# Cached values multiplied four pages at a visit in the four column quarters, the second recurrence begun three ticks later, and two steps of VectorE reordered

## The chip, the core and the metric
The kernel runs on one core of a Trainium2 chip. TensorE (matrix products), VectorE, ScalarE and GpSimd compute, SyncE issues the DMAs, and all five run their own instruction streams and wait for each other by semaphores. The metric is the time of the whole launch on the device in microseconds (us), the median of several runs.

## What is computed
One step of a hybrid decoder layer, for a prompt of 1024 tokens and for 8 running sequences (samples) with one new token each. Both go through a combined input projection, a gated linear recurrence (4 heads, in blocks), a differential attention (4 heads, two query and key pairs each), an output projection and a feed-forward with squared relu. The change concerns the samples' attention over their cached values:

```python
def diff_attn_sample(q, k_new, v_new, k_past, v_past, lam):
    # q, k_new (Bd,1,H,2,DH); v_new (Bd,1,H,DV); k_past (Bd,P,H,2,DH); v_past (Bd,P,H,DV)
    s_past = einsum('bqhcd,bkhcd->bhcqk', q, k_past) * scale
    s_new = einsum('bqhcd,bkhcd->bhcqk', q, k_new) * scale
    p = softmax(concatenate([s_past, s_new], -1))
    a = p[:, :, 0] - lam * p[:, :, 1]
    return (einsum('bhqk,bkhv->bqhv', a[..., :P], v_past)
            + einsum('bhqk,bkhv->bqhv', a[..., P:], v_new))

k_past = cache_k[l, page_table].reshape(Bd, past, H_DIFF, 2, DH_DIFF)
v_past = cache_v[l, page_table].reshape(Bd, past, H_DIFF, DV_DIFF)
```

There are 8 sequences of 16 pages, a page is 128 positions of 512 numbers (256 KB), so 128 pages of values are fetched through the page table and multiplied by the softmax's coefficients.

## The kernel before
**Main line.** Everything is float32; dense products are split into high and low parts and done as three products each (`split_matmuls`, L85 to L87). The `front` computes the input projection in groups (kinds dq, low, gk, gq, gv, dk, dv, gg; nine groups for a kind of 512 columns: eight token tiles and the samples). Then `feed_forward` runs for the first half of the tokens (part A: output projection, then eight groups of four up tiles and eight down outputs), then for the second half (part B). For part A TensorE has two PSUM banks for its dense results, so it can't begin an output before VectorE has taken the one two places earlier (for down outputs that is the residual addition, L2195).

**Ticks.** Main work is cut into ticks. In the front a token tile is two ticks, a sample tile one. In feed-forward A an output tile and an up tile are two ticks and each of the eight down outputs is one; up tile x of group g holds the ticks 16 + 16g + 2x and the next, and the down outputs start at tick 24 + 16g. Every engine walks the same ticks in order, and at each calls `beside(tick)`, which runs one step of each side job that the table in `program` (L2801 to L2835) has put there, in the order of the `put` lines. So an engine's instruction order is fixed by hand, and an engine that waits inside a side step holds up its main work behind it. In a down product TensorE does its first two outputs and then both first ticks' side work together (L1976 to L1983), while VectorE does each tick's side work ahead of the addition of that output (L2189 to L2195).

**Side jobs that matter here.** `recurrence` (parts A and B, 4 chunks of 9 phases each, one phase a tick): VectorE subtracts decays in phases 0 and 1, multiplies in phases 3 to 5 (`multiply(c, 0..2)`, L1165), and copies masked scores out of PSUM in phases 5 to 7 (`pick(c, 0..2)`, L1183); TensorE does the score levels in phases 5, 6 and 7 (L1284), of which phase 6 waits for pick 0 and the second multiply and phase 7 for pick 1 and the third multiply, and sums outputs in phase 8, after pick 2. `cached_keys` (`keysA`, `keysB`): SyncE fetches key pages, GpSimd multiplies them with the queries (L2338), VectorE sums (L2327). `sample_recurrence`, then `sample_softmax` (L2344), then `cached_values` (L2456), which starts as the softmax ends. In the front, `sample_normed("dk")` (L794) norms the samples' keys on VectorE after GpSimd has taken the roots; SyncE stores them to `k_sample` (L331) and waits for that norm, two groups behind.

**Cached values.** A unit is two pages. SyncE fetches one unit a step into a ring of three slots (L2207). TensorE visits it two steps later: two products of 128 x 32 coefficients (`a_pad`, four heads padded to 32 columns) with 512 columns of values, in quarters g and g + 1 of the array's columns (L2550 to L2552), so the quarters' sums stand in the partitions 32g to 32g + 31 of one bank. Eight units are one sequence. After them VectorE masks the bank (L2530, `vm`), TensorE adds it over the partitions by a product with ones (`total`, L2538), and VectorE adds the row to `acc_s` (L2515).

## Time and profile before
| | |
|---|---|
| three runs | 1525.34 us median (1522.49 to 1526.05) |
| profiled execution, whole | 1533.14 us |
| its span, first to last instruction | 1531.2 us |
| mean granted TensorE clock | 0.971 of full |
| busy: TensorE products, VectorE, ScalarE, GpSimd | 94%, 56%, 35%, 21% |
| cached-value products, L2551 | 256 records, 769.8 to 1055.5 us |
| DMA | 212 MB, 138 GB/s over the span |

Times inside an execution are microseconds from its first instruction. PE is TensorE, PEld its weight loads, DVE VectorE, ACT ScalarE, POOL GpSimd, SPq the DMA issues of SyncE. A float32 product of two unsplit operands leaves two records. Products are pipelined and their ends are modelled, so records overlap and starts tell more than durations. The profiled execution is one of the kernel, and its time is compared with itself.

### The profile page before, as it was taken

How to read it: one execution, taken by the hardware profiler on the slowest of the kernel's cores; microseconds unless marked ns; L12 is line 12 of the kernel's file. 1: busy time of each engine (PE TensorE's matmuls, PEld its weight loads, DVE VectorE, ACT ScalarE, POOL GpSimd, SP SyncE). 2: the span in 40 equal slices, each digit the busy share in tenths (PEclk: the TensorE clock that was granted, in tenths of full speed). 3: DMA queues.
4: the chain of work that ended last, by engine and by line, in shares of the span. 5: the costliest groups of instructions: out<-in, count | busy, mean ns of one | idle time of the engine just before them, and what ended most of it. 6: DMA issues, size and time to landing. Idle time of an engine off the chain costs nothing.

```text
span 1531.2 us, 23353 instructions
## 1 busy us (share of the span) xinstructions
PE 1438.9 (94%) x8649; PEld 1165.9 (76%) x8649; DVE 857.8 (56%) x1438; ACT 533.5 (35%) x980; POOL 324.6 (21%) x366
## 2 busy tenths in 40 slices
PE   6998899889999989999899999999899999999997
PEld 5767677667776767876666665556899999999997
DVE  4467667744647776786746472425255544455542
ACT  5462232314545564520413140303244322233321
POOL 2456624523412523464000000000030000000000
PEclk9999999989999999999899999999999999999999
DMA  7547644434244532463437464844153312233211
GB/s 240 152 145 210 209 140 151 131 115 119 71 144 134 162 130 90 161 220 116 156 112 246 140 227 133 296 138 152 49 177 120 106 63 81 83 110 111 102 38 57
DMA packets 115635, 211.99 MB, mean 138 GB/s; under 512 B 12665, under 2 KB 45722, under 8 KB 115522
## 3 DMA queue, kind: packets, MB, share of 16 engines
q1 hardware_dynamic: 115522, 210.50, 42.4%
q8 instruction: 69, 1.13, 0.3%
q14 instruction: 44, 0.36, 0.1%
HBM read 184.00 MB, written 26.46 MB: 137 GB/s over the span
## 4 chain that ended last, share of the span: by engine, by line
PE 66%; DVE 5%; ACT 2%; issue 2%; DMA 1%; SPq 0%; ACTq 0%; DVEq 0%
PE ps L85 18%; PE ps L87 17%; PE ps L86 17%; PE ps L2551 4%; PE ps L1465 2%; PE ps L1502 2%; PE ps L1284 1%; DVE uw_l L2038 1%; PE ps L1486 1%; DMA out_y_prompt<-y 1%; ACT uw_h L2034 1%; DVE dl L2126 0%; PE ps L2612 0%; PE ps L2538 0%; PE ps L1692 0%
## 5 line engine op out<-in xcount | busy, mean ns | idle before, releaser
L85 PE MATMUL ps<-uh,dh 128*128 128x512 f32 (+2 forms) x768 | 253.8, 330 | 18.1 <-DVE dl L2126 10.6
L87 PE MATMUL ps<-uh,dl 128*128 128x512 f32 (+2 forms) x768 | 248.5, 324 | 0.0
L86 PE MATMUL ps<-ul,dh 128*128 128x512 f32 (+2 forms) x768 | 247.9, 323 | 0.0
L2338 POOL TENSOR_TENSOR kr<-kr,qb 128x512 f32<-128x512 f32 x128 | 174.3, 1378 | 123.7 <-DMA kr<-in_cache_k 119.7
L2195 DVE TENSOR_TENSOR xt<-xt,ps 128x256 f32<-128x256 f32 (+2 forms) x192 | 97.2, 511 | 167.0 <-PE ps L87 166.2
L85 PEld LDWEIGHTS ps<-uh,dh 128*128 128x128 f32 x768 | 146.2, 190 | 46.9 <-DVE xt L2195 22.3
L2049 ACT ACTIVATE dh<-raw_dn 128x1024 fp32r<-128x1024 f32 x64 | 67.1, 1049 | 266.2 <-PE ps L87 263.3
L87 PEld LDWEIGHTS ps<-uh,dl 128*128 128x128 f32 x768 | 146.2, 190 | 12.1
L86 PEld LDWEIGHTS ps<-ul,dh 128*128 128x128 f32 x768 | 146.6, 191 | 10.0
L85 PE MATMUL ps<-x2hB,uw_h 128*128 128x264 f32 (+1 forms) x512 | 145.9, 285 | 3.2 <-DVE uw_l L2038 2.6
L2034 ACT ACTIVATE uw_h<-raw_up 128x1024 fp32r<-128x1024 f32 x80 | 84.4, 1055 | 182.8 <-PE ps L87 182.7
L86 PE MATMUL ps<-x2lB,uw_h 128*128 128x264 f32 (+1 forms) x512 | 145.2, 284 | 0.0
L87 PE MATMUL ps<-x2hB,uw_l 128*128 128x264 f32 (+1 forms) x512 | 145.0, 283 | 0.0
L2038 DVE TENSOR_TENSOR uw_l<-raw_up,uw_h 128x1024 fp32r<-128x1024 f32 x80 | 101.6, 1270 | 43.1 <-ACT uw_h L2034 43.1
L85 PE MATMUL ps<-x2hA,uw_h 128*128 128x512 f32 x256 | 106.9, 418 | 0.0
L87 PE MATMUL ps<-x2hA,uw_l 128*128 128x512 f32 x256 | 101.3, 396 | 0.0
L86 PE MATMUL ps<-x2lA,uw_h 128*128 128x512 f32 x256 | 100.9, 394 | 0.0
L85 PEld LDWEIGHTS ps<-x2hB,uw_h 128*128 128x128 f32 x512 | 97.2, 190 | 3.7 <-DVE uw_l L2038 2.8
L2327 DVE TENSOR_REDUCE sd<-kr 128x8 f32<-128x512 f32 x128 | 84.7, 675 | 25.3 <-POOL kr L2338 25.2
L86 PEld LDWEIGHTS ps<-x2lB,uw_h 128*128 128x128 f32 x512 | 97.1, 190 | 0.0
L87 PEld LDWEIGHTS ps<-x2hB,uw_l 128*128 128x128 f32 x512 | 96.9, 189 | 0.0
L2126 DVE TENSOR_TENSOR dl<-raw_dn,dh 128x1024 fp32r<-128x1024 f32 x64 | 80.3, 1254 | 27.3 <-ACT dh L2049 27.2
(327 smaller groups left out, 2888.0 us busy)
## 6 DMA issues: line engine op xcount, KB each, us to landing
kr<-in_cache_k SPq DMA_DIRECT2D x128, 256.0 KB, 3.2
raw_up<-in_w_up_units SPq DMA_DIRECT2D x64, 512.0 KB, 3.7
raw_dn<-in_w_down SPq DMA_DIRECT2D x64, 512.0 KB, 4.6
vr<-in_cache_v SPq DMA_DIRECT2D x128, 256.0 KB, 3.1
raw<-in_w_in_units SPq DMA_DIRECT2D x24, 512.0 KB, 5.1
raw_up<-in_w_out_units SPq DMA_DIRECT2D x16, 512.0 KB, 3.6
xin<-in_x_prompt SPq DMA_DIRECT2D x8, 512.0 KB, 5.5
xt_scratch<-xts SPq DMA_DIRECT2D x8, 512.0 KB, 5.8
```

Of the source, the lines that this page charges most:

```text
L85: pe.matmul(out, lh, rh, start=first and n == 0, stop=False)
L86: pe.matmul(out, lh, rl, start=False, stop=False)
L87: ins = pe.matmul(out, ll, rh, start=False, stop=last and n == len(ks) - 1)
L1465: pe.matmul(ps[:, score_bank(n, c) + j // 512, 0:x], qt[r, b, i * P:(i + 1) * P], kt[r, b, j:j + x], start=True, stop=j + x < w)
L2034: act.activation(uw_h[:, t % 2, :, :], raw_up[:, t % 2, :].rearrange("p (k c) -> p k c", c=P), ACT.Copy).then_inc(up_high, 1)
L2038: dve.tensor_tensor(uw_l[:, t % 2, :, :], raw_up[:, t % 2, :].rearrange("p (k c) -> p k c", c=P), uw_h[:, t % 2, :, :].bitcast(FP32), ALU. ...
L2049: act.activation(dh[:, x, :], raw_dn[:, x % 2, :], ACT.Copy).then_inc(dn_high, 1)
L2126: dve.tensor_tensor(dl[:, x, :], raw_dn[:, x % 2, :], dh[:, x, :].bitcast(FP32), ALU.subtract).then_inc(dn_low, 1)
L2195: dve.tensor_tensor(xt[:, o, c], xt[:, o, c], ps[:, bank("down", g, o, p), 0:spans[p][1]], ALU.add).then_inc(added, 1)
L2327: dve.tensor_reduce(m["sd"][:, b, g, :], place(v)[:, :].rearrange("p (h d) -> p h d", d=DH), X, ALU.add).then_inc(k_used, 1)
L2338: pool.tensor_tensor(k[:, :], k[:, :], qb[v // PAGES][:, :], ALU.mult).then_inc(k_multiplied, 1)
L2551: ins = pe.matmul(ps[32 * g:32 * g + 32, 2 + b % 2, :], a_pad[:, b % 2, 2 * l + j, :], vring[v % VRING][:, j, :], start=l < 2, stop=l >= 6 ...
```

## The change
`cached_values` fetches and visits four pages at a time. A unit is now four pages, 32 units in all, in a ring of eight single-page places. SyncE fetches two pages of a unit at an even step and two at the following odd step; TensorE visits a unit at step 2u + 3 with four products, one in each quarter; masking, total and addition stand at steps 10, 11 and 12 + 8b instead of 9, 10 and 10 + 8b. The places of the ring reach over memory that other jobs used, so SyncE waits for three more things before it starts and, before page 7, for the softmax's last step. The job has 69 steps instead of 68.

In `recurrence`, both parts, the third multiply moves behind the first pick of the same phase. In the front, the norm of the samples' keys moves from the first to the second group of dv. In the table the tail of `keysB` is spread over 16 ticks instead of 15, the softmax and values start one tick later, and `recurB` starts 13 ticks after the softmax's start instead of 10, with its first load 10 instead of 7 after; counted from the feed-forward's start recurB begins at tick 72 instead of 68. Two places in memory move by 64 bytes. The diff, with the moved memory places left out:

```diff
--- before.py
+++ after.py
@@ -889,7 +889,7 @@
                     gkq_sample(g)
             if g in (START["gg"] + 3, START["gg"] + 4):
                 m["late"]["vector"](dve, g - START["gg"] - 3)
-            if x == 0 and kind in ("low", "dv"):
+            if kind == "low" and x == 0 or kind == "dv" and x == 1:
                 sample_normed("dq" if kind == "low" else "dk")
             if ticks_of(g) == 2:
                 beside(TICK[g] + 1)
@@ -1219,10 +1219,12 @@
             if ph == 2 and c > first:
                 finish(c - 1)
             if here:
-                if 3 <= ph < 6:
+                if 3 <= ph < 5:
                     multiply(c, ph - 3)
                 if 5 <= ph < 8:
                     pick(c, ph - 5)
+                if ph == 5:
+                    multiply(c, 2)
             yield
 
     def scalar(act):
@@ -2200,15 +2202,9 @@
 
-VALUE_UNITS = NS * PAGES // 2
+VALUE_UNITS = NS * PAGES // 4
 KEY_PAGES = NS * PAGES // 2
-VRING = 3
-
-
-def load_unit(sp, cache, m, slot, arrived, first):
-    for j in range(2):
-        page = sp.value_load(m["pages"][0:1, first + j:first + j + 1], min_val=0, max_val=NPOOL - 1)
-        sp.dma_start(slot[:, j, :], cache[bass.ds(page, 1), :, :].rearrange("a p n -> p (a n)")).then_inc(arrived, 16)
+VRING = 2
 
@@ -2455,7 +2451,9 @@
 
 def cached_values(nc, a, m, ps, sem, at):
 
-    vring = [at(f"vr{i}", 166.625 + 4 * i, [P, 2, W]) for i in range(VRING)]
+
+    places = [164.6875 + 2 * i for i in range(7)] + [202.625]
+    vring = [at(f"vr{i}", x, [P, W]) for i, x in enumerate(places)]
     a_pad = at("a_pad", 9.75, [P, 2, PAGES, 32])
     hmask = at("hmask", 1.5, [P, W])
     vm = at("vm", 162.6875, [P, W])
@@ -2466,17 +2464,26 @@
     keys_in = [16 * len([v for v in range(2 * KEY_PAGES) if key_sem(v) == i]) for i in range(VRING)]
     v_used, v_masked, v_totalled, v_added, padded = (sem(x) for x in ("v_used", "v_masked", "v_totalled", "v_added", "padded"))
     sums = m["head_sums"][:, 0:H]
-    STEPS = VALUE_UNITS + 4
+    STEPS = 2 * VALUE_UNITS + 5
 
     def sync(sp):
         sp.wait_ge(sem("scored"), 4 * UNITS)
         sp.wait_ge(sem("product_made"), 2 * UNITS)
         sp.wait_ge(sem("k_used"), 2 * KEY_PAGES)
+        for i in range(3):
+            sp.wait_ge(sem(f"od_out{i}"), (96, 80, 80)[i])
+        sp.wait_ge(sem("st_updated"), 1)
         for s in range(STEPS):
-            if s < VALUE_UNITS:
-                if s >= VRING:
-                    sp.wait_ge(v_used, s - VRING + 1)
-                load_unit(sp, a["cache_v"], m, vring[s % VRING], v_in[s % VRING], 2 * s)
+            u, j = divmod(s, 2)
+            if u < VALUE_UNITS:
+                if j == 0 and u >= VRING:
+                    sp.wait_ge(v_used, u - VRING + 1)
+                for v in (4 * u + 2 * j, 4 * u + 2 * j + 1):
+                    if v == 7:
+                        sp.wait_ge(v_added, 1)
+                    page = sp.value_load(m["pages"][0:1, v:v + 1], min_val=0, max_val=NPOOL - 1)
+                    sp.dma_start(vring[v % 8][:, :], a["cache_v"][bass.ds(page, 1), :, :].rearrange("a p n -> p (a n)"))\
+                        .then_inc(v_in[u % VRING], 16)
             yield
 
     def gpsimd(pool):
@@ -2503,12 +2510,12 @@
                     dve.wait_ge(sem("coef_made"), 1)
                     dve.wait_ge(sem("fill_steps"), 6)
                 if b >= 2:
-                    dve.wait_ge(v_used, 8 * (b - 1))
+                    dve.wait_ge(v_used, 4 * (b - 1))
                 dve.tensor_copy(a_pad[:, b % 2, :, 0:H], coef[:, b, :, :]).then_inc(padded, 1)
-            b, j = divmod(s - 9, 8)
+            b, j = divmod(s - 10, 8)
             if j == 0 and 0 <= b < NS:
                 v_masked_now(dve, b)
-            b, j = divmod(s - 10, 8)
+            b, j = divmod(s - 12, 8)
             if j == 0 and 0 <= b < NS:
                 dve.wait_ge(v_totalled, b + 1)
                 dve.wait_ge(v_added, b + 1)
@@ -2524,7 +2531,7 @@
                           sums.unsqueeze(2).to_broadcast([NS, H, DV]), ALU.mult).then_inc(sem("ods_done"), 1)
 
     def v_masked_now(dve, b):
-        dve.wait_ge(v_used, 8 * (b + 1))
+        dve.wait_ge(v_used, 4 * (b + 1))
         if b:
             dve.wait_ge(v_totalled, b)
         dve.tensor_tensor(vm[:, :], ps[:, 2 + b % 2, :], hmask[:, :], ALU.mult).then_inc(v_masked, 1)
@@ -2538,20 +2545,19 @@
             pe.matmul(ps[0:NS, 2 + b % 2, :], m["ones"][:, 0:NS], vm[:, :], start=True, stop=True).then_inc(v_totalled, 1)
 
         for s in range(STEPS):
-            v = s - 2
-            if 0 <= v < VALUE_UNITS:
-                b, l = divmod(v, 8)
-                pe.wait_ge(v_in[v % VRING], keys_in[v % VRING] + 32 * (v // VRING + 1))
+            u, j = divmod(s - 3, 2)
+            if j == 0 and 0 <= u < VALUE_UNITS:
+                b, l = divmod(u, 4)
+                pe.wait_ge(v_in[u % VRING], keys_in[u % VRING] + 64 * (u // VRING + 1))
                 if l == 0:
                     pe.wait_ge(padded, b + 1)
                     if b >= 2:
                         pe.wait_ge(v_added, b)
-                for j in range(2):
-                    g = (2 * l + j) % 4
-                    ins = pe.matmul(ps[32 * g:32 * g + 32, 2 + b % 2, :], a_pad[:, b % 2, 2 * l + j, :],
-                                    vring[v % VRING][:, j, :], start=l < 2, stop=l >= 6, tile_position=(0, 32 * g))
+                for g in range(4):
+                    ins = pe.matmul(ps[32 * g:32 * g + 32, 2 + b % 2, :], a_pad[:, b % 2, 4 * l + g, :],
+                                    vring[(4 * u + g) % 8][:, :], start=l == 0, stop=l == 3, tile_position=(0, 32 * g))
                 ins.then_inc(v_used, 1)
-            b, j = divmod(s - 10, 8)
+            b, j = divmod(s - 11, 8)
             if j == 0 and 0 <= b < NS:
                 total(b)
             yield
@@ -2824,13 +2830,13 @@
         put("attnB", [t0 + i for i in range(ATTEND_STEPS + 1) if i != norm])
         late = t0 + ATTEND_STEPS + 1
         put("keysB", [t0 + 2 + 41 * i // 25 for i in range(25)])
-        put("keysB", [late + 15 * i // (side["keysB"]["steps"] - 25) for i in range(side["keysB"]["steps"] - 25)])
-        t1 = late + 15
-        put("loadRB", [t1 + 7])
+        put("keysB", [late + 16 * i // (side["keysB"]["steps"] - 25) for i in range(side["keysB"]["steps"] - 25)])
+        t1 = late + 16
+        put("loadRB", [t1 + 10])
         put("sgla", [late + 1 + i * 3 // 2 for i in range(side["sgla"]["steps"])])
         put("soft", range(t1, t1 + side["soft"]["steps"]))
         put("values", range(t1 + 12, t0 + FEED_TICKS))
-        put("recurB", range(t1 + 10, t1 + 10 + side["recurB"]["steps"]))
+        put("recurB", range(t1 + 13, t1 + 13 + side["recurB"]["steps"]))
         put("mixload", [t1 + 54])
         put("mixB", [t0 + 137 + i // 2 for i in range(9)])
 
```

## Rows read from the trace of the kernel before
**Rows 1.** The page: the chain that ended last, by line.
```profile
PE ps L85 18%; PE ps L87 17%; PE ps L86 17%; PE ps L2551 4%; PE ps L1465 2%; PE ps L1502 2%; PE ps L1284 1%; DVE uw_l L2038 1%; PE ps L1486 1%; DMA out_y_prompt<-y 1%; ACT uw_h L2034 1%; DVE dl L2126 0%; PE ps L2612 0%; PE ps L2538 0%; PE ps L1692 0%
```

**Rows 2.** TensorE's waits over the span: us in total, times, longest us.
```profile
PE ps L1284 <- DVE at_sb L1193: 13.1, 2, 8.6
PE ps L85 <- DVE dl L2126: 10.6, 2, 6.8
PE ps L85 <- DVE xt L2195: 7.9, 5, 2.9
```

**Rows 3.** The chain in order of time, feed-forward A: start us, us, what.
```profile
769.91 0.99 PE ps L2551 x8
1018.65 0.98 PE ps L2551 x4
1022.61 0.98 PE ps L2551 x4
```

**Rows 4.** Timeline of TensorE at a down product's first ticks, 844 to 852 us.
```profile
844.90 0.40 PE L85 MATMUL ps<-uh,dh 128*128 128x512 f32 x1
...
845.61 0.39 PE L85 MATMUL ps<-uh,dh 128*128 128x512 f32 x1
...
846.39 1.07 PE L2551 MATMUL ps<-vr,a_pad 128*32 128x512 f32 x8
847.27 1.02 PE L2538 MATMUL ps<-vm,ones 128*8 128x512 f32 x2
851.18 0.51 PE L85 MATMUL ps<-uh,dh 128*128 128x512 f32 x1 [2.88 <-DVE xt L2195]
```

**Rows 5.** Windows: busy by engine, then PEclk, DMA share, GB/s.
```profile
186.00:197.00 11.00, 8.19 (x43) 7.13 (x44) 5.10 (x10) 0.00 (x0) 0.60 (x1) 0.53 0.47 135
...
306.30:319.80 13.50, 9.07 (x46) 7.36 (x46) 7.24 (x14) 0.00 (x0) 1.29 (x1) 0.50 0.35 100
...
757.00:767.00 10.00, 5.43 (x13) 4.28 (x14) 7.08 (x19) 5.43 (x6) 0.95 (x1) 0.50 0.71 229
...
852.40:855.70 3.30, 3.30 (x10) 2.05 (x11) 2.15 (x9) 0.00 (x0) 0.00 (x0) 0.50 0.71 234
...
964.00:996.00 32.00, 32.00 (x132) 19.70 (x131) 15.55 (x18) 11.70 (x15) 0.00 (x0) 1.00 0.84 296
```

**Rows 6.** Timeline of VectorE before the down product at 761 us.
```profile
754.94 1.76 DVE L1151 TENSOR_TENSOR e<-g_in 128x256 f32<-128x256 f32 x5
...
760.28 1.23 DVE L2126 TENSOR_TENSOR dl<-raw_dn,dh 128x1024 fp32r<-128x1024 f32 x1 [1.46 <-ACT dh L2049]
```

**Rows 7.** Timeline of VectorE in the front, recurrence chunks 0 and 3.
```profile
184.44 2.31 DVE L1177 TENSOR_TENSOR e<-e,g_in 128x128 f32<-128x128 f32 x2
...
302.29 4.18 DVE L798 TENSOR_TENSOR zs<-zs,zsum 8x512 f32<-8x512 f32 x1 [1.55 <-POOL zsum L683]
306.51 1.63 DVE L800 TENSOR_TENSOR zs<-zs,gains 8x512 f32<-8x512 f32 x1
```

**Rows 8.** Timeline of GpSimd, 302 to 308 us.
```profile
302.23 5.36 POOL L2338 TENSOR_TENSOR kr<-kr,qb 128x512 f32<-128x512 f32 x4
```

**Rows 9.** Timeline of VectorE in chunk 2 of the front's recurrence.
```profile
260.38 0.49 DVE L1177 TENSOR_TENSOR e<-e,g_in 128x128 f32<-128x128 f32 x2
...
261.12 0.73 DVE L1191 COPY_PREDICATED at_sb<-lmask,ps 128x512 f32<-128x512 int32 x1
261.89 0.94 DVE L1193 COPY_PREDICATED at_sb<-lmask,ps 128x256 f32<-128x256 int32 x2
```

**Rows 10.** Timeline of GpSimd at the same time.
```profile
261.09 2.53 POOL L2338 TENSOR_TENSOR kr<-kr,qb 128x512 f32<-128x512 f32 x2
```

**Rows 11.** Value page fetches (L2211), 770 to 1056 us: who waited; landing.
```profile
  PEld ps L2551: 0.4, 1
...
DMA to landing us min/median/max: 2.5/3.1/5.6
```

**Rows 12.** Timeline of ScalarE, fifth group of dv.
```profile
340.93 0.69 ACT L561 ACTIVATE st<-ps,r 128x512 f32<-128x512 f32 x1 [10.58 <-DMA out_v_prompt<-st]
```

More of the change, by code:

```diff
@@ L1032, in recurrence @@
     first, last = CHUNKS * part, CHUNKS * (part + 1)
-    base = (166.625, 178.625)[part]
+    base = (166.625, 178.6875)[part]
     g_in = at(f"g_in{part}", base, [P, 3, 2, P])
@@ L1633, in mixing @@
         tiles = [(t, half) for t in range(4) for half in range(2)] + [(4, 0), (4, 1)]
-        rowsB = at("rowsB", 178.625, [P, MIX_RING, W])
+        rowsB = at("rowsB", 178.6875, [P, MIX_RING, W])
     else:
```

## The prediction
> **What bounds the kernel now.** I read the page first. The chain that ended last is mostly TensorE's: its split products at L85 to L87 and then, at 4% of the span, the cached-value products at L2551 [rows 1]. So a microsecond of TensorE's own work is worth a microsecond, if nothing else is late. Next I read TensorE's waits, to see where it stands still [rows 2]. Three kinds touch the change: two waits of the recurrence's score products on the predicated copies of VectorE (13.1 us, the longest 8.6), two waits on the split of the down weights (10.6 us, the longest 6.8), and waits on VectorE's residual additions (7.9 us). The windows then show what each wait costs beyond itself: behind the long ones the granted clock is 0.50, the lower of its two levels (1.2 of 2.4 GHz), while TensorE works [rows 5].
>
> **Four pages at a visit.** Before, 64 units of two pages are visited. In four places, at the first two ticks of a down product, two units are visited back to back, so there are 60 stretches. Two neighbouring single visits start 3.96 us apart [rows 3] with twelve dense products between. Three dense products take 0.71 us, from 844.90 to 845.61 [rows 4], and twelve 2.81, so a visit takes 1.15 us: 0.98 on the chain [rows 3], and 0.17 for entering and leaving it. After the change there are 32 visits of four. Their price stands in the trace: a back-to-back pair of units touches all four quarters (l even: quarters 0 and 1, then 2 and 3), and its eight records run from 846.39 to 847.27, 0.88 us until the next product starts [rows 4]. Another such place, 769.91, had 0.99 on the chain [rows 3]. I take 1.00. The work itself falls from 60 x 0.98 = 58.8 to 32.0 us. Entering and leaving is paid once per tick that has side work. Before, each of the 60 is such a tick. After, I count 32 visits, 8 ticks with a recurrence step alone and one total alone: 41. That saves 19 x 0.17 = 3.2 us. Term one: -30.0 (bounds -27 and -31).
> The Trainium skill speaks against the full price: TensorE: Matmul & The Clock Gate, section Measured speedup vs the span model, lists 3.07x for four row tiles and 2.38x for three column tiles of 512 columns, and says that the two tilings agree closely. By that, four together would take 1.30 times one product alone; with this case's single product (0.85 us) a visit would cost 1.11, and the change would save 3.5 us less. The rows above are of this kernel, and the sum goes by them.
>
> **The totals move off the boundary.** A tick is half an up tile or one of the eight outputs of a down product, 12 dense products each. Values started at tick 70 of the feed-forward and start at 71; VectorE adds batch b's total at step 12 + 8b instead of 10 + 8b. A down product's first tick is 72 + 16k. Before, odd b lands there exactly: VectorE sits in the wait for TensorE's total before it does the first residual addition, and TensorE, with two banks, can't go on: 2.88 us at 851.18 [rows 4], two more of 2.7 and 1.4 in the sum of rows 2, with 0.4 at the end. After the first the clock is at half for 3.3 us [rows 5], after the second as long: 1.7 lost each time. After the change steps 20, 36 and 52 are ticks 91, 107 and 123, inside the down product, and only the masking (step 18, 34, 50) falls on its second tick, with a whole product of cover. Gain 7.4 + 3.4 = 10.8.
> But TensorE does both first ticks of a down product together, and the moved recurrence (first step at tick 72, before 68) now has steps 32 and 33 there (phases 5 and 6 of its last chunk): phase 6 waits for the first pick, three predicated copies of 0.73 and 0.94 us together [rows 9], with nothing between: 1.8. Steps 16 and 17 (phases 7 and 8) wait for one short copy: 0.4. The total of even b comes one tick after a masking that stands behind VectorE's work on an up tile: 0.1 to 0.3 each. Term two: -10.8 + 2.8 = -8.0 (-5 to -9).
>
> **Recurrence away from the softmax.** Before tick 72 VectorE has the last softmax steps, the recurrence's first two (five of their subtractions alone take 1.76 us), and ScalarE has the exponentials of those, in front of the last down split, which ends at 761.5 [rows 6]; TensorE waits 6.8 us and then runs 5.4 us at half clock, 2.7 lost [rows 2, 5]. After, softmax ends at tick 71 and the recurrence starts at 72, so some 5 us of VectorE's work and two exponentials leave the way to the split. Rebuilt with the same durations the split ends within 0.3 us of TensorE's need. What is late next: the last softmax step, a weight split and the recurrence's first step stand before the first residual addition. With that tile's own steps they are about 8 us (2.2 + 2.2 + 1.2 + 1.7 + 0.7), and TensorE has two outputs of 2.8 us of products to cover them: a new stall of 2.6, perhaps with some half clock. Term three: -9.5 + 2.6 + 0.9 = -6.0 (-3 to -9). SyncE's new waits cost nothing: the stored rows and the state update ended long before, and the wait at page 7 for the softmax's last sum comes two ticks after it with no weight load behind it for six ticks.
> **Keys over 16 ticks instead of 15.** By tick 54 VectorE has made two reductions fewer (0.68 us each) before the other split on which TensorE waits, for 3.8 us (10.6 less 6.8 [rows 2]); the half clock that follows may shorten. Term four: -2.0 (0 to -4).
>
> **The last multiply behind the first pick.** In phase 5 of both recurrences TensorE's phase 6 needs the pick, and the last multiply only phase 7. In chunk 0 the multiply stands first and takes 2.31 us for two instructions [rows 7] that take 0.49 elsewhere [rows 9]; with its last part (0.4 us) that is 2.6 ahead of the pick, which could start at 184.44. A pick isn't slowed by GpSimd's products: at 261.12 it takes its 0.73 beside them [rows 9, 10]. TensorE's wait of 4.5 (13.1 less 8.6) falls to 2.0. Behind it 8.19 us of work ran at 0.53 [rows 5], 4.1 lost; a wait of 2.0 may or may not lower the clock, I take half. Term five: -2.6 - 2.4 = -5.0 (-2.6 to -6.7).
> **The samples' key norm one group later.** It stood in front of the pick of chunk 3. Its two instructions took 4.18 and 1.63 us [rows 7], beside GpSimd's four key products, 5.36 us [rows 8]. TensorE waited 8.6, and ran 9.07 us at 0.50, 4.5 lost [rows 2, 5]: 13.1. After: the pick ends near 302.4 (wait 0.3). The multiply now meets GpSimd's products and, priced by 4.18 for one such instruction at worst, ends by 306.3 to 308.3; a reduction and the second pick (2.17) follow, and phase 7 waits 2 to 4 us. With 3.0 for that and 1.7 for some half clock, 5.0 is lost instead of 13.1. Term six: -8.0 (-4 to -11). SyncE now waits for this norm with the store of the samples' keys, until about 311 to 312 instead of 308; it is priced as a rival.
>
> **Sum.** 30 + 8 + 6 + 2 + 5 + 8 = 59. The profiled execution took 1533.1 us (span 1531.2), so 1474 for one like it; the three runs have a median of 1525.3, 7.8 below, and the same difference gives 1466.
>
> **The rivals.**
> (a) Four streams don't run together when they start at once, and a visit of four costs two products. For: each quarter needs its own stream of 512 columns. Against: rows 4. Price 32 x 0.9 = 29: 1495.
> (b) The front doesn't keep its 13 us. SyncE stays in the norm's wait; behind it stand a key store, a page load and the value store whose landing ScalarE already waited for once, 10.6 us until 340.93, which cost TensorE 1.9 [rows 12]. For: TensorE arrives 8 us earlier, SyncE 3 later. Against: that later wait hangs on the recurrence's end, which moves along. 1479.
> (c) The softmax stall comes back in full, at the first residual addition: 1466 + 8 = 1474.
> (d) Slower: the visit waits for its second pair of pages. SyncE issues it a tick later than the first, behind its waits for the weight splits, and the visit comes two ticks after. Landing takes 3.1 us, at most 5.6 [rows 11]; the up stages already use 0.84 of the DMA engines at 296 GB/s [rows 5], and shorter ticks want about a sixth more. I count about 5 us of slack. The gain is gone once every one of 32 visits waits 59 / 32 = 1.85 us, so from a lateness of about 7 us on; with 2.2 us each it is 1466 + 70 = 1536. Against: before, with the same two pages a tick, the visits waited 0.4 us in all for pages [rows 11].
>
> **How the numbers follow.** Forecast 1466, chance 0.63, with 1454 to 1478 as its own range from the terms' bounds; (c) 0.12; (b) 0.13; (a) 0.06; (d) 0.03; the rest, smaller give-backs up to no change, 0.03. The range to 1486 takes in (c) and (b) and leaves out (a), (d) and the rest. A measurement can tell about 0.3% (4.6 us) from no change. Faster 0.96, same 0.01, slower 0.03.
>
> **What would show it.** L2551 in 32 places with eight records each, the next product 0.9 to 1.0 us after the first; no wait of L85 on the residual addition near the middle of the feed-forward but one of under 2 us where the recurrence's phases 5 and 6 meet; the wait on the down split after the softmax gone, a shorter one on the addition behind it; the waits on the predicated copies at 2 and at under 4 us; fewer windows at 0.50. Visits near 1.9 us would prove (a); waits of L2551 on the pages (d); a longer wait of ScalarE's L561 on the value store (b).

## The result and the profile after

| | kernel before | changed kernel |
|---|---|---|
| median | 1525.69 us (1522.49 to 1530.10, 4 runs) | 1490.01 us (1484.83 to 1492.57, 4 runs) |
| ratio | | 0.976, 95% interval 0.972 to 0.980 |
| profiled execution, whole | 1533.14 us | 1487.50 us |
| its span | 1531.2 us | 1485.6 us |

The change is faster by 36 us. The forecast was 1466 with a range to 1486, so the sign is right and the time lies outside the range. Between the two profiled executions 45.6 us went, where the sum had 59. The medians differ by less, 36 us, because the profiled execution of the kernel before was 7.8 us above its median and that of the changed kernel 2.5 below. So the miss is 13 us in the traces and 23 us in the medians; both are taken apart below.

The new kernel's lines stand a few places off: L2557 is the cached-value product (L2551 before), L2197 the residual addition, L2128 the split of the down weights, L1286 the recurrence's score product, L2485 the page fetch.

First the visits. TensorE's timeline around one of them (start us, us, what), which answers to [rows 3, 4]:

```profile
930.12 0.40 PE L87 MATMUL ps<-x2hA,uw_l 128*128 128x512 f32 x1
930.45 1.06 PE L2557 MATMUL ps<-vr,a_pad 128*32 128x512 f32 x8
931.45 0.50 PE L85 MATMUL ps<-x2hA,uw_h 128*128 128x512 f32 x1
```

Four pages hold the stream for 1.00 us, as priced. TensorE's waits over the span (us in total, times, longest us) answer to [rows 2]:

```profile
PE ps L1286 <- DVE at_sb L1193: 7.2, 4, 3.1
...
PE ps L2557 <- DMA vr<-in_cache_v: 6.0, 3, 4.1
...
PE ps L85 <- DVE dl L2128: 4.1, 2, 2.8
PE ps L85 <- DVE xt L2197: 4.1, 3, 2.9
```

The waits on the predicated copies fell from 13.1 to 7.2, those on the down split from 10.6 to 4.1, those on the residual addition from 7.9 to 4.1. The line of L2557 is new: 6.0 us of waiting for value pages, where there were 0.4 [rows 11]. What the waits drag behind them is in the windows (from:to, us, busy by engine with counts, then PEclk, DMA share, GB/s), which answer to [rows 5]:

```profile
181.00:190.00 9.00, 7.00 (x48) 5.43 (x46) 5.91 (x13) 0.69 (x1) 2.48 (x2) 0.81 0.51 135
301.00:309.50 8.50, 5.44 (x25) 4.03 (x24) 7.25 (x13) 1.63 (x2) 0.21 (x1) 0.69 0.19 41
...
805.80:816.00 10.20, 7.84 (x40) 5.25 (x41) 3.57 (x13) 1.33 (x2) 0.00 (x0) 0.51 0.95 356
898.00:904.80 6.80, 6.30 (x38) 5.67 (x39) 4.75 (x11) 0.00 (x0) 0.00 (x0) 0.51 0.46 147
964.00:996.00 32.00, 32.00 (x152) 20.54 (x150) 10.96 (x16) 4.22 (x5) 0.00 (x0) 1.00 0.58 171
```

Two new stretches at the lower clock level (0.51) stand in the feed-forward, at 806 and at 898 us. To find where the 45.6 us came from, I cut both traces at the same pieces of work, the starts of named additions on VectorE. Worked out from the records: length of the stage, and in brackets how long TensorE had nothing running, then half of what it ran at half clock (what the half clock cost).

```
                      start to      part A, g0 o4   g2 o4 to       g3 o4 to        to the end of
                      g0 o4         to g2 o4        g3 o4          end of part A   TensorE's work
before                593.5 (75.9)  129.3 ( 7.9)    64.0 (6.8,2.7) 297.6 ( 7.4,3.4) 439.4
changed               581.4 (62.7)  126.9 ( 5.3)    54.0 (4.6,1.7) 280.2 (10.1,7.2) 437.8
changed, once more    581.3 (62.5)  127.1 ( 5.5)    56.6 (4.6,4.6) 280.7 ( 9.7,8.2) 438.0
```

(The first two columns have both losses in one number; "g3 o4" is the fifth down output of the fourth group. Some of the recurrence's own work moved from the third column to the fourth with its start.) In the feed-forward's part A, TensorE's work without the losses went from 462.7 to 432.2, by 30.5 us: that is the visits. Its losses went from 28.2 to 28.9, where the prediction took 16 off. That is where the traces' 13 us are missing: 16.7 here, of which 3.3 came back elsewhere.

Not all of the 45.6 us belong to the change. Two runs below have one half of the kernel before each. The four pages alone have the old front, and their trace reaches g0 o4 after 588.8 us with 70.8 lost, against 593.5 with 75.9; their waits on the predicated copies there were 3.2 and 7.0 us, where the trace that the prediction read had 4.5 and 8.6. The norm alone has the old code behind the front, and takes 443.4 us from the end of part A to the end of the span, where the kernel before takes 446.7 and the changed one 443.1. So about 8 us of what the profiled execution of the kernel before lost, it lost in stretches where the same code lost less in another execution.

### The profile page after: what moved, and what is told of

The parts are those of the page before. It is cut to its first block, busy times and chain, and to the rows that moved or that the text cites. A ratio compares the mean times of both kernels' runs of the same rounds, so it can differ in the third digit from the quotient of the medians.

```text
span 1485.6 us, 23355 instructions
## 1 busy us (share of the span) xinstructions
PE 1406.0 (95%) x8649; PEld 1161.6 (78%) x8649; DVE 857.0 (58%) x1438; ACT 533.8 (36%) x980; POOL 324.3 (22%) x366
## 4 chain that ended last, share of the span: by engine, by line
PE 63%; DVE 6%; ACT 3%; issue 2%; DMA 1%; SPq 1%; POOL 0%; ACTq 0%; DVEq 0%; POOLq 0%
PE ps L85 18%; PE ps L87 17%; PE ps L86 17%; PE ps L1467 2%; PE ps L2557 2%; PE ps L1504 2%; PE ps L1286 1%; DVE uw_l L2040 1%; PE ps L1488 1%; DMA vr<-in_cache_v 1%; ACT uw_h L2036 1%; DMA out_y_prompt<-y 1%; DVE dl L2128 1%; PE ps L2618 0%; PE ps L2010 0%
## 5 line engine op out<-in xcount | busy, mean ns | idle before, releaser
L2197 DVE TENSOR_TENSOR xt<-xt,ps 128x256 f32<-128x256 f32 (+2 forms) x192 | 97.4, 511 | 157.9 <-PE ps L87 157.3
L2036 ACT ACTIVATE uw_h<-raw_up 128x1024 fp32r<-128x1024 f32 x80 | 84.5, 1056 | 172.8 <-PE ps L87 172.7
L2128 DVE TENSOR_TENSOR dl<-raw_dn,dh 128x1024 fp32r<-128x1024 f32 x64 | 81.6, 1275 | 27.9 <-ACT dh L2051 27.7
L2179 DVE SCALAR_TENSOR_TENSOR xr<-ps,rb 128x256 f32<-128x256 f32 (+1 forms) x96 | 49.0, 514 | 83.1 <-PE ps L87 82.8
```

What stands on the lines that cost most here:

```text
L2036: act.activation(uw_h[:, t % 2, :, :], raw_up[:, t % 2, :].rearrange("p (k c) -> p k c", c=P), ACT.Copy).then_inc(up_high, 1)
L2128: dve.tensor_tensor(dl[:, x, :], raw_dn[:, x % 2, :], dh[:, x, :].bitcast(FP32), ALU.subtract).then_inc(dn_low, 1)
L2179: dve.scalar_tensor_tensor(vt[:, i % 2, 0:spans[p][1]], ps[:, bank("up", g, x, p), 0:spans[p][1]], 0.0, rb2[:, tokens(p)], ALU.max, ALU.mu ...
L2197: dve.tensor_tensor(xt[:, o, c], xt[:, o, c], ps[:, bank("down", g, o, p), 0:spans[p][1]], ALU.add).then_inc(added, 1)
```

## The long wait near 808 us

SyncE's issues in the changed kernel (start us, us, what):

```profile
792.92 1.77 SPq L2485 DMA_DIRECT2D vr<-in_cache_v  x2
800.37 0.33 SPq L1117 DMA_DIRECT2D kept_og<-go  x1
800.75 0.43 SPq L1831 DMA_DIRECT2D raw_up<-in_w_up_units  x1
801.22 0.45 SPq L1843 DMA_DIRECT2D raw_dn<-in_w_down  x1
802.42 1.45 SPq L2485 DMA_DIRECT2D vr<-in_cache_v  x2
```

VectorE and TensorE at the same place:

```profile
799.59 0.75 DVE L1207 SCALAR_TENSOR_TENSOR go<-gate,hr,go 128x512 f32<-128x512 f32 x1
...
808.16 1.94 PE L2557 MATMUL ps<-vr,a_pad 128*32 128x512 f32 x8 [4.14 <-DMA vr<-in_cache_v]
```

A unit's first two pages are issued at 792.9, its other two at 802.4. Between them SyncE stands in the wait of the recurrence's store (L1117, phase 2) for the gated rows `go`, which VectorE ends at 800.34; SyncE goes on at 800.37. The waits of SyncE from 790 to 806 us name it (us, times, longest):

```profile
SPq L1117 <- DVE go L1207: 5.7, 1, 5.7
```

TensorE was ready at 804.0. Before the change this store fell on tick 79; the recurrence's start, four ticks later, puts it on tick 83, between the two halves of a unit. This is theory S. The store's wait itself is not new. The trace of the kernel before, from 770 to 1060 us, has it at three of the four stores, up to 7.7 us long, and it did no harm there, since both pages of a unit were issued in one step:

```profile
SPq L1117 <- DVE go L1207: 18.1, 3, 7.7
```
 The rival, D, is that the DMA engines are simply full there (0.95 of them busy, 356 GB/s), and pages would be late whatever SyncE did.

## Experiments

The kernel before ran on the same chip beside them: its medians were 1527.3 us for the first four kernels, 1528.0 for the next four (two quarters, the parts alone) and 1527.9 for the last four. Times of one kernel scatter by up to 7 us about the median, so differences of medians under about 3 us tell nothing, and there the traces are compared.

### The changed kernel once more, and the store moved

> The changed kernel once more, as the level for the three runs beside it: 1490, ratio to before 0.976. In its trace the pages of one visit are waited for 4.1 us near 808 us, behind SyncE's wait of 5.7 us for the gated rows of the recurrence (L1117), and 8.5 us are lost to half clock and 9.9 to standing still between 762 and 1042 us.

Measured: 1491.73 us, ratio 0.9753 (0.9731 to 0.9774). Its trace has the same pages missing (6.0 us in 3 waits, the longest 3.4), 9.7 us idle and 8.2 us of half clock in the table's stage from g3 o4 to the end of part A.

```diff
-            if part and ph == 3 and here:
+            if part and ph == 5 and here:
                 ... (waits, then the gate's load)
-            if part and ph == 2 and c > first:
+            if part and c > first and (ph == 5 and here or ph == 2 and not here):
                 sp.wait_ge(og_gated, c)
                 sp.dma_start(a["og"][(c - 1) * P:c * P, :], go[:, :]).then_inc(go_out, 16)
```

> The changed kernel, with SyncE's store of the recurrence's gated rows and the load of the next gate (phases 2 and 3) moved to phase 5. Theory S: the second pair of pages came late at 808 us because SyncE stood 5.7 us in the wait of that store, which the later start of the recurrence moved to tick 83, between the two pairs of a unit. Then the wait of 4.1 us and the half clock behind it (5.1 us) go: 9 us less than after_again, 1481. Rival D: the pages are late because the DMA engines are full there (360 GB/s, share 0.99); then the wait stays at 3 to 4 us and the time is the same, 1489 to 1491.

Measured: 1482.15 us, ratio 0.9697 (0.9679 to 0.9714), 9.6 less than the changed kernel beside it. The window over that place, and the visit in it:

```profile
801.00:811.00 10.00, 9.99 (x65) 7.24 (x64) 9.57 (x26) 5.40 (x7) 0.00 (x0) 1.00 0.90 325
```
```profile
805.85 1.07 PE L2557 MATMUL ps<-vr,a_pad 128*32 128x512 f32 x8
```

No wait, full clock, and the DMA engines nearly as busy as in the changed kernel (0.90, 325 GB/s). The stage from up tile x2 of group 4 to the third down output behind it took 22.3 us instead of 30.1. Rival D falls as the cause of the long wait. But there was nothing to spare either: the last page of that unit was issued at 801.82, landed at 805.80, and the visit began at 805.85. The landings of this pair took 4.0 and 4.4 us, those of the changed kernel 4.6 and 4.7, against a median of 3.1 before the change [rows 11]. The prediction had counted some 5 us of slack at each visit.

### All four pages at the even step

```diff
-                for v in (4 * u + 2 * j, 4 * u + 2 * j + 1):
+                for v in range(4 * u, 4 * u + 4) if j == 0 else ():
```

> The changed kernel, with all four pages of a unit issued at the even step instead of two and two, so that they stand ahead of the store's wait in SyncE's order and ahead of the next weight loads. Theory S: the wait at 808 us goes, and the small ones of 0.7 and 1.2 us at 883 and 946 too, each with its half clock where it has some: 9 to 11 us less than after_again, 1480. Rival D: four pages in one burst fill the DMA engines as much, and delay weights: no gain, 1489 to 1492, perhaps with new waits for raw_up or raw_dn.

Measured: 1479.06 us, ratio 0.9672 (0.9651 to 0.9694), 12.7 less. The store's wait is still there (5.1 us near 800 us), but the pages stand ahead of it. TensorE's waits from 760 to 1050 us:

```profile
PE ps L85 <- DVE dl L2128: 2.0, 1, 2.0
PE ps L1286 <- DVE at_sb L1193: 1.9, 1, 1.9
PE ps L85 <- DVE xt L2197: 1.2, 2, 0.7
```

Not one wait for a page is left. So two different edits, one that moves the wait and one that moves the pages, both take the long wait away, and the second takes the two smaller page waits (0.7 to 1.5 us near 885 and 948) as well. No store stands between the halves of those two units, and the run with the moved store kept both waits (0.6 and 2.1 us); what made their pages late is not shown beyond this, that an earlier issue removes it.

### The recurrence back at tick 68

```diff
-        put("loadRB", [t1 + 10])
+        put("loadRB", [t1 + 6])
-        put("recurB", range(t1 + 13, t1 + 13 + side["recurB"]["steps"]))
+        put("recurB", range(t1 + 9, t1 + 9 + side["recurB"]["steps"]))
```

> The changed kernel, with the second recurrence (and its first load) begun at tick 68 of the feed-forward as in the kernel before, instead of 72; all else stays. Theory S: the softmax's stall comes back (6.8 us and half clock, 7 to 8 us net of the residual wait of 2.9 that goes), but the store's wait falls on tick 79 again, so the pages at 808 us are on time (9 us less), and phases 5 and 6 no longer share a down product's first ticks (1.9 us and 3.4 us of half clock less): in sum 6 us less, 1484. As the prediction had it (shift worth 6, its price 2.8): 3 us more, 1493.

Measured: 1483.55 us, ratio 0.9701 (0.968 to 0.9721), 8.2 less than the changed kernel. Its waits from 735 to 1050 us:

```profile
PE ps L85 <- DVE dl L2128: 6.2, 1, 6.2
PE ps L2557 <- DMA vr<-in_cache_v: 3.2, 2, 1.8
PE ps L85 <- DVE xt L2197: 2.8, 3, 1.5
PE ps L2368 <- DVE small L2409: 1.8, 1, 1.8
```

The softmax's stall is back (6.2 us at 753.76), and the stage with it takes 62.6 us instead of 56.6; but the stages behind it take 265.4 instead of 280.7. The store falls on tick 79 again. That is between the two halves of a unit too, but SyncE found its rows ready there. The third store, at tick 97, is between halves and did wait, 5.9 us, and the visit of that unit waited for its pages:

```profile
872.22 0.33 SPq L1117 DMA_DIRECT2D kept_og<-go  x1
874.27 1.44 SPq L2485 DMA_DIRECT2D vr<-in_cache_v  x2
879.00 1.07 PE L2557 MATMUL ps<-vr,a_pad 128*32 128x512 f32 x8 [1.39 <-DMA vr<-in_cache_v]
```

So the harm needs both, a place between the halves and a result that is late; and it still depends on TensorE: the changed kernel's third store waited 5.4 us between the halves at 885 us, and the visit, at 893.7, found its pages there.

The two places where the shift loses can be told apart in their stages: 7.8 us near 808, by the run with the moved store, and near 900 (from the third up tile to the fifth down output of group 5) losses of 7.2 us where there are none with the recurrence at 68. There the recurrence's phases 5 and 6 share the down product's first two ticks. So the part of the change that the prediction valued at 6 us of gain, 3.2 after the 2.8 that it charged in its totals' term, cost 8.

### Two quarters instead of four

```diff
+                    q = g if l == 0 else g % 2
-                    ins = pe.matmul(ps[32 * g:32 * g + 32, ...], ..., start=l == 0, stop=l == 3, tile_position=(0, 32 * g))
+                    ins = pe.matmul(ps[32 * q:32 * q + 32, ...], ..., start=l == 0, stop=(l == 3 and g > 1) or (l == 0 and g > 1),
+                                    tile_position=(0, 32 * q))
```

> The changed kernel, with the last three visits of every four putting their four pages in two quarters (0, 1, 0, 1) instead of four; the sums over the partitions come out the same. If the price of a visit is set by the columns each quarter has to take, 24 visits cost about 1.85 us instead of 0.995: 20 us more than the changed kernel, 1512. If it is set by the issue of eight records or by entering and leaving the tick, nothing changes: 1491.

Measured: 1501.87 us, ratio 0.9827 (0.9805 to 0.9849), 10 more than the changed kernel. A visit of this kernel in two quarters, with the product behind it:

```profile
937.21 1.91 PE L2558 MATMUL ps<-vr,a_pad 128*32 128x512 f32 x8
939.05 0.50 PE L85 MATMUL ps<-x2hA,uw_h 128*128 128x512 f32 x1
```

1.84 us instead of 1.00, in 24 places: 20.2 us of work, so rival (a) of the prediction is refuted by what its world looks like. The time rose by half of that only. The losses behind the fifth down output of group 3 fell from 17.9 to 10.3 us: slower visits leave SyncE and the pages more time, and the long wait near 810 was 2.3 instead of 3.4 us with a shorter half clock. That reading is not tested by itself; it would be the effect that took gain from the change, seen from its other side.

### The parts alone

```diff
-            if x == 0 and kind in ("low", "dv"):
+            if kind == "low" and x == 0 or kind == "dv" and x == 1:
```

> The kernel before with one edit: the norm of the samples' keys one group of dv later. The prediction priced it at 8.0 us, between 4 and 11; by the trace of the changed kernel (waits of 8.6 and the half clock behind them against 0.3 and 3.1) it is worth 6.3: 1521 against 1527. Rival (b) of the prediction: SyncE and the store of the prompt's values give it back, the wait of ScalarE at 340 us grows by as much: 1527, no change.

Measured: 1517.64 us, ratio 0.9922 (0.9898 to 0.9945), 10.4 less than before: more than the trace of the changed kernel had. At the place of the 8.6 us a wait of 1.03 is left, with no half clock behind it:

```profile
301.43 1.78 PE L1284 MATMUL ps<-e 64*128 64x64 f32 x28 [1.03 <-DVE at_sb L1193]
301.00:311.00 10.00, 9.57 (x78) 7.97 (x79) 7.01 (x12) 1.63 (x2) 5.18 (x5) 1.00 0.40 137
```

The wait of ScalarE for the value store is 10.60 us as before [rows 12], so rival (b) is refuted.

> The kernel before with one edit: the third multiply behind the first pick, in both recurrences. The prediction priced it at 5.0 us, between 2.6 and 6.7; by the trace of the changed kernel 4.8: 1522.5 against 1527. Rival: it is given back at the next wait that has another cause (the front's norm, 8.6 us at 302 us, grows): 1527.

(The diff is the part of the change in `recurrence`.) Measured: 1521.64 us, ratio 0.995 (0.9933 to 0.9968), 6.4 less than before. The wait of chunk 3, 8.57 us before, is 7.83 here, not longer (in the trace of the next run, whose front is that of the kernel before, it is 7.03), so the rival finds no support.

> The changed kernel without the two reordered steps of VectorE and with the second recurrence begun at tick 68: only four pages at a visit, the ring, the totals' steps and the table's one tick. By the prediction's terms one, two (without its new stall of 2.8) and four: 30 + 10.8 + 2 = 43 us less than before, 1484. By the run with the recurrence at 68, whose stages give 33 us from the middle of the feed-forward on: 33 to 36 us less, 1492 to 1494; the waits for pages (3.2 us) and for a residual addition (1.5) then stand where the totals' waits stood.

(The changed kernel with `sample_normed`, `multiply` and the start of recurB as before.) Measured: 1492.38 us, ratio 0.977 (0.9748 to 0.9792), 35.6 less than before. The sum of the terms, 43, lies outside the interval (32 to 38 us). Its trace has waits that had no place in that sum: for pages 1.5 and 1.3 us, for a residual addition 1.5, in the softmax 1.8, 6.1 us in all.

Alone, the three give 10.4 + 6.4 + 35.6 = 52.4; together, with the recurrence at tick 68, 43.8. The norm and the multiply, worth 16.8 alone, add 8.2 to the four pages (10.5 by the ratios, each uncertain by 4 to 5). Two of the parts hinder each other, and VectorE's timelines show where. Chunk 3 of the front's recurrence in the changed kernel, with GpSimd beside it:

```profile
295.37 0.92 DVE L1193 COPY_PREDICATED at_sb<-lmask,ps 128x256 f32<-128x256 int32 x2
296.19 5.18 DVE L1177 TENSOR_TENSOR e<-e,g_in 128x128 f32<-128x128 f32 x2
```
```profile
296.18 5.03 POOL L2334 TENSOR_TENSOR kr<-kr,qb 128x512 f32<-128x512 f32 x4
```

The same with the norm's edit alone, where the multiply stands ahead of the pick:

```profile
298.87 0.48 DVE L1177 TENSOR_TENSOR e<-e,g_in 128x128 f32<-128x128 f32 x2
299.28 0.41 DVE L1180 TENSOR_TENSOR e<-e,g_in 128x256 f32<-128x256 f32 x1
299.61 0.72 DVE L1191 COPY_PREDICATED at_sb<-lmask,ps 128x512 f32<-128x512 int32 x1
```

Behind the pick, the two instructions start together with GpSimd's key products and take as long as these, 5.18 us instead of 0.48; TensorE waits 3.1 us for the pick that follows, where 1.03 are left with the norm's edit alone. Ahead of it they are done before GpSimd begins. With the half clock behind the 3.1 (1.7 to 3.4 us) that makes 4 to 5 us of what the two lose in company; the rest is within the uncertainty. The Trainium skill has the rule in SBUF — State Buffer, section SBUF: two separate sides: a VectorE instruction with both inputs in SBUF and a GpSimd instruction that reads SBUF shut each other out for a whole instruction. These rows agree in that VectorE was shut out and the copies from PSUM were not. But it was for more than one instruction: by the single records VectorE's first took 3.88 us, over three of GpSimd's, its second 1.38, and GpSimd's own took 1.26 to 1.33 throughout.

### Putting the pieces together

Four kernels, each the changed kernel with more of the edits. First the recurrence three ticks later still, at 75:

```diff
-        put("loadRB", [t1 + 10])
+        put("loadRB", [t1 + 13])
-        put("recurB", range(t1 + 13, t1 + 13 + side["recurB"]["steps"]))
+        put("recurB", range(t1 + 16, t1 + 16 + side["recurB"]["steps"]))
-        put("mixload", [t1 + 54])
+        put("mixload", [t1 + 57])
```

> The changed kernel, with the second recurrence (and its first load) three ticks later again, at tick 75, and the load behind it three ticks later. Theory S: the store's wait falls on tick 86 behind both pairs of a unit, so the pages at 808 us are on time (8 us less); no chunk has phases 5 and 6, or 6 and 7, in a down product's first two ticks, so the wait of 1.9 us at 900 us goes with its half clock and the small wait before it (7.5 us less, as in the run at tick 68); and the residual wait of 2.3 to 2.9 us behind the softmax loses the recurrence's first steps (1 to 2 us less): 1474 to 1476. Rival: what matters is only that the recurrence overlaps the values' pages, wherever it stands; then one of the waits stays in another place and the time is 1482 to 1486.

Measured: 1480.96 us, ratio 0.97 (0.9676 to 0.9724), 5 above what was expected. The stage of the softmax behaved (52.2 us, 4.6 lost), the wait of 1.9 us near 900 is gone; but a wait of 2.8 us for a down split stands at 807 us, one of 1.5 for a residual addition at 887, and pages are waited for 3.3 us. The rival was half right: the recurrence's steps meet something wherever they stand. (Its profiled execution, 1476.25 us, was 4.7 below the median, so the trace shows less than was lost.)

> recur_at_75 with all four pages of a unit issued at the even step. Theory S: what page waits are left in recur_at_75 (2 to 3 us, as in the run at 68 and in the one with the later store) go: 2 to 3 us less than recur_at_75, 1472. Rival D: nothing, as a burst of four lands as late.

Measured: 1477.0 us, ratio 0.9674 (0.9646 to 0.9701), 4.0 less; the page waits are 0.3 us.

The other two also give the third multiply its place by chunk:

```diff
-                if 3 <= ph < 5:
+                if 3 <= ph < 5 or ph == 5 and c:
                     multiply(c, ph - 3)
                 if 5 <= ph < 8:
                     pick(c, ph - 5)
-                if ph == 5:
+                if ph == 5 and c == 0:
                     multiply(c, 2)
```

> all_four_75 with two more edits: the third multiply stands behind the pick only in the first chunk of the front's recurrence, ahead of it in all others, and the store of the gated rows is in phase 5. The norm's edit alone gave 10 us and left no wait at 302 us, while both edits together left one of 3.1 us, in which the multiply's two short instructions took 5.2 us beside GpSimd's key products, against 0.48 in front of the pick. So 3.1 us and a half clock (1.7 to 3.4) less than all_four_75: 1467. If the 10 us of the norm's edit alone were chance, 1472.

> best_c with the store of the gated rows where the change has it, in phase 2. With four pages issued ahead, the store's wait (5.1 us in the run with four at once) delays only the weight loads, for which TensorE did not wait there: the same time as best_c within 1 us. If a weight load is late, a wait for a split appears and best_c is 2 us faster.

Measured: 1474.72 us, ratio 0.9658 (0.9637 to 0.9679), with the store in phase 5, and 1471.1 us, ratio 0.9633 (0.9612 to 0.9655), with the store in phase 2. Both miss 1467, but that number was built on an expected 1472 for the kernel with four pages at once, which took 1477.0. The last kernel differs from that one in the multiply's place alone and is 5.9 us faster, where 5 were expected. In both the wait of 3.05 us at the front's chunk 3 is one of 1.03, the one that the norm's edit alone had left, and no half clock follows it:

```profile
301.24 1.00 PE L1286 MATMUL ps<-e 64*128 64x64 f32 x14 [1.03 <-DVE at_sb L1193]
```

The intervals of the last two overlap, so whether the store's place still matters once the pages stand ahead isn't settled; it isn't worth 2 us in the direction expected. The last kernel is 56.8 us faster than the kernel before and 18 faster than the changed one (0.9633 / 0.9753 = 0.988, each against the kernel before beside it).

## Why the prediction was wrong, point by point

**What the medians say of the sum.** Each part can be read from two kernels that differ in it alone, each against the kernel before beside it:

| | forecast | measured |
|---|---|---|
| four pages, totals, keys (the four pages alone) | 30 + 10.8 + 2 = 42.8 | 35.6 |
| norm and multiply, on top of these | 13 | 8.2 |
| recurrence from tick 68 to 72, on top of both | 6 - 2.8 = 3.2 | -8.2 |
| sum | 59 | 35.6 |

So 23 us are missing: 7 in the first line, 5 in the second, 11 in the third. Each measured part is uncertain by 3 to 5 us, so the second line could be noise; the first and third can't. The bullets below give the mechanisms, from the traces.

**Four pages at a visit: right.** 30.0 forecast, 30.5 in the trace; a visit 1.00, as priced from the back-to-back pair of the kernel before. The figures of the Trainium skill (TensorE: Matmul & The Clock Gate, section Measured speedup vs the span model), 3.07 for four row tiles and near agreement of the two tilings, gave the prediction's estimate of 1.11; the trace disagrees with that here. Counted like a visit, up to the start of the next dense product, one float32 product alone (the total at 938.23) holds the stream for 0.95:

```profile
938.23 1.02 PE L2545 MATMUL ps<-vm,ones 128*8 128x512 f32 x2
939.18 0.50 PE L85 MATMUL ps<-x2hA,uw_h 128*128 128x512 f32 x1
```

So four pages in four quarters cost 0.05 more than one product. (Four times the 0.71 us of three products is 2.84 and not 2.81, which takes 0.6 us off the term and changes nothing.)

**The totals and the moved recurrence: the step that failed.** The term said -8.0 (-5 to -9). The totals' three stalls went as worked out, and the wait where phases 5 and 6 meet came with 1.87 us against 1.8:

```profile
882.59 1.06 PE L2557 MATMUL ps<-vr,a_pad 128*32 128x512 f32 x8 [0.66 <-DMA vr<-in_cache_v]
887.95 0.50 PE L85 MATMUL ps<-uh,dh 128*128 128x512 f32 x1 [1.32 <-DVE dl L2128]
898.50 3.68 PE L1286 MATMUL ps<-e 64*128 64x64 f32 x32 [1.87 <-DVE at_sb L1193]
```

But the losses behind that stage's start rose by 6.5 us instead of falling by 8. The new ones: pages, 6.0 us of waiting and some 4 of half clock; the half clock behind the 1.87, another 3; a split wait of 1.3 ahead of it. The term priced the wait between the phases and not what follows it, though the same text had charged half clock behind every wait that it took away. And of the moved recurrence it followed only the steps on VectorE and TensorE. Its steps on SyncE were left out: the sentence "SyncE's new waits cost nothing" covered the waits that the diff adds, not the one that it moves. With that one wait out of the way the stage near 808 us was 7.8 us shorter.

**Rival (d) had the place and not the cause.** It named the second pair of pages, issued a tick later, and counted some 5 us of slack behind the waits for weight splits. That count left out the store's wait, 5.7 us by itself, and it was too high even without it: with the store moved, 0.05 us were left at this visit. It also asked for lateness at all of 32 visits to matter, so it got 0.03; one visit of 32 that is late by 4.1 us, with its half clock, was worth 8 to 10 us, which was enough to leave the range.

**The softmax: a little under.** -6.0 (-3 to -9) forecast; the loss in its stage fell by 3.2 in one execution and by 0.3 in the other, so by the second it lies outside its own bounds. The wait behind the stall came as foreseen (2.87 against 2.6); a wait of 1.78 for the softmax's reduction at 736 us was not seen (it is there with the recurrence at 68 too, so the shift didn't make it), and the half clock was 1.7 or 4.6 where 0.9 was taken. Rival (c), the stall in full, is refuted by the 2.87. That the shift as a whole loses 8 us is the sum of this term and of the failed one.

**Keys: right as far as it can be told** (-2.0 against -2.4 in the column from g0 o4 to g2 o4; the other kernels with this edit have 126.0 to 128.8 us there, where it was 129.3). **Multiply and norm: right in the two profiled executions** (-13.0 against -12.1 up to g0 o4), and 8.2 by the medians, with 13 not excluded. Both terms were priced from waits of one execution that ran 7.8 us above the median; against the trace with the old front above, the changed front gained 7.4. Term six, 8.0, came out as 10.4 alone and, by the trace of the changed kernel, some 6 in company, with the multiply among GpSimd's products, as the term's own working had it (2 to 4 us of waiting; 3.06 measured).

So, by the traces, a sum of 59 lost 16.7 us in part A of the feed-forward, and 3.3 came back elsewhere: 0.5 at the visits and 3.7 in part B and behind its last product, less 0.9 in the front. The 3.7 are not the change's, since the run with the norm alone has them too.

**From the sum to the time.** The prediction took its 59 us off one execution, which had run 7.8 us above the median, and assumed that the changed kernel's would stand as far above its median. It stood 2.5 below, and that is the other 10 us of the miss. The range was too narrow besides: 1478 is not the far end of the terms' bounds, which add up to 42 us and so to 1484, and 1490 lies outside that as well.

## What to carry to other kernels

When a side job moves by some ticks, list its steps on every queue, the DMA issuing one first, and write down what stands behind each of its waits in the new place: a store that waits for a result is harmless inside one stage and stops a just-in-time fetch in another. Issue such fetches ahead of any wait in the same tick. And if steps of VectorE are reordered one by one, look again at what GpSimd does at the new time, since two good orders can be bad together.

## What the runs showed of the hardware

The granted clock does not follow a wait's length alone. The same wait of 2.87 us at the same place of the same program was followed by full clock in the one profiled execution of the changed kernel and by the lower level in the other. The wait and the window behind it, first the one:

```profile
752.43 0.47 PE L85 MATMUL ps<-uh,dh 128*128 128x512 f32 x1 [2.87 <-DVE xt L2197]
```
```profile
752.50:759.30 6.80, 6.80 (x33) 4.62 (x34) 3.96 (x13) 3.46 (x4) 0.00 (x0) 1.00 0.21 57
```

and the other:

```profile
752.52 0.77 PE L85 MATMUL ps<-uh,dh 128*128 128x512 f32 x1 [2.87 <-DVE xt L2197]
```
```profile
752.50:759.30 6.80, 6.78 (x21) 4.17 (x22) 3.43 (x11) 3.54 (x4) 0.00 (x0) 0.57 0.02 8
```

Three microseconds hang on that, at a wait that nothing in the program changed; a wait of 2.85 us at 807 us did the same in two of the last kernels (clock 0.62 from 805 to 813 us in one, 1.00 in the other). So for waits of 2 to 3 us the cost of the half clock behind them is a range and not a number (0 to 3 us here).

The quarters of the columns run together and a quarter's own streams don't: four pages took 1.00 us in four quarters and 1.84 in two, and one product alone 0.95.
